# A three-layer block in split fp32r: sums over later keys as two fp32r passes, high passes first after a norm, another order of the feed-forward and of the first loads

## The reference

```python
z = einsum("bqhd,bkhd->bhqk", q, k) * scale
log_beta = log_sigmoid(z)
log_fail = where(s_idx < t_idx, log_beta - z, 0.0)          # = -softplus(z)
survive = cumsum(log_fail, axis=3, reverse=True) - log_fail # sum over later keys
a = where(s_idx < t_idx, exp(log_beta + survive), 0.0)
o = einsum("bhqk,bkhd->bqhd", a, v)
```

```python
u, g = split(rms_norm(h) @ w_up_gate)
u = causal_dwconv(u, conv_w_ffn)          # three taps over tokens
ffn = (gelu(u) * g) @ w_down
```

## Time and profile before

| | us |
|---|---|
| median of 3 runs | 868.92 (868.86 to 870.4) |
| the profiled execution, its own time | 868.39 |
| its span, first to last instruction | 866.6 |
| PE busy | 841.5 |
| DVE busy | 613.7 |
| ACT busy | 490.8 |
| POOL busy | 145.1 |

### The profile page before, as it was taken

One profiled execution on the slowest core, in us unless ns is written; L12 is line 12 of the kernel. 1 busy time (PEld: TensorE's weight loads), 2 busy tenths in 40 slices (PEclk: granted clock), 3 DMA queues, 4 the chain that ended last, 5 costly groups with the idle time before them and its releaser, 6 DMA issues.

```text
span 866.6 us, 16776 instructions
## 1 busy us (share of the span) xinstructions
PE 841.5 (97%) x6768; PEld 803.8 (93%) x6768; DVE 613.7 (71%) x1004; ACT 490.8 (57%) x814; POOL 145.1 (17%) x151
## 2 busy tenths in 40 slices
PE   7999999999999999999999999789999999999996
PEld 6999999999999989999999999789999999888886
DVE  6647787886666686767764478797887697568754
ACT  6345556445444565555564458558777555346654
POOL 0000000000000333333341121335434011000002
PEclk9999999999999999999999999899999999999998
DMA  9654424436666524665566624435544376654431
GB/s 338 210 153 128 158 98 158 135 112 180 192 178 190 175 87 155 194 187 181 174 193 215 191 82 155 163 124 176 183 147 154 115 217 184 186 171 143 123 98 49
DMA packets 39853, 139.81 MB, mean 161 GB/s; under 512 B 4432, under 2 KB 5600, under 8 KB 39648
## 3 DMA queue, kind: packets, MB, share of 16 engines
q1 hardware_dynamic: 37728, 135.71, 49.8%
q10 hardware_dynamic: 2048, 3.02, 1.0%
HBM read 137.65 MB, written 1.06 MB: 160 GB/s over the span
## 4 chain that ended last, share of the span: by engine, by line
PE 79%; DVE 12%; ACT 4%; POOL 3%; issue 1%; DMA 1%; DVEq 0%; SPq 0%; ACTq 0%; POOLq 0%
PE ps L1593 62%; PE ps L1596 5%; DVE weights_lo L984 4%; PE ps L1618 3%; PE ps L1690 1%; DVE arena L1204 1%; DVE arena L1176 1%; PE ps L1680 1%; POOL arena L441 1%; PE ps L1705 1%; PE ps L1960 1%; PE ps L1942 1%; DMA raw_weights<-weights_in 1%; DVE x_lo L1171 1%; POOL arena L462 1%
## 5 line engine op out<-in xcount | busy, mean ns | idle before, releaser
L1593 PE MATMUL ps<-x_hi,weights_hi 128*128 128x256 f32 (+3 forms) x1288 | 374.5, 291 | 6.3 <-DVE x_lo L999 2.8
L984 DVE TENSOR_TENSOR weights_lo<-raw_weights,weights_hi 128x1024 fp32r<-128x1024 f32 x252 | 311.7, 1241 | 92.9 <-ACT weights_hi L549 92.8
L1593 PE MATMUL ps<-x_lo,weights_hi 128*128 128x256 f32 (+3 forms) x1288 | 364.6, 283 | 0.0
L1593 PE MATMUL ps<-x_hi,weights_lo 128*128 128x256 f32 (+3 forms) x1288 | 364.1, 283 | 0.0
L549 ACT ACTIVATE weights_hi<-raw_weights 128x1024 fp32r<-128x1024 f32 x252 | 264.8, 1053 | 163.5 <-issue 71.0
L1593 PEld LDWEIGHTS ps<-x_hi,weights_hi 128*128 128x128 f32 x1288 | 244.1, 190 | 14.3 <-issue 7.0
L1593 PEld LDWEIGHTS ps<-x_lo,weights_hi 128*128 128x128 f32 x1288 | 244.3, 190 | 1.0 <-issue 0.7
L1593 PEld LDWEIGHTS ps<-x_hi,weights_lo 128*128 128x128 f32 x1288 | 244.4, 190 | 0.0
L1593 PE MATMUL ps<-y_hi,weights_hi 128*128 128x256 f32 (+1 forms) x488 | 137.8, 282 | 1.4 <-POOL y_lo L445 1.4
L1593 PE MATMUL ps<-y_lo,weights_hi 128*128 128x256 f32 (+1 forms) x488 | 137.4, 282 | 0.0
L1593 PE MATMUL ps<-y_hi,weights_lo 128*128 128x256 f32 (+1 forms) x488 | 137.1, 281 | 0.0
(11 more groups left out here) (230 smaller groups left out, 1075.0 us busy)
## 6 DMA issues: line engine op xcount, KB each, us to landing
raw_weights<-weights_in SPq DMA_DIRECT2D x252, 512.0 KB, 3.7
arena<-decay_rows ACTq DMA_DIRECT2D x8, 256.0 KB, 3.9
masks<-masks_in SPq DMA_DIRECT2D x1, 1379.0 KB, 11.0
hidden<-xT_in SPq DMA_DIRECT2D x2, 272.0 KB, 3.6
hidden<-xT_in SPq DMA_DIRECT2D x1, 544.0 KB, 6.2
raw_weights<-weights_in SPq DMA_DIRECT2D x2, 256.0 KB, 4.3
out<-arena SPq DMA_DIRECT2D x4, 128.0 KB, 2.2
out<-arena ACTq DMA_DIRECT2D x4, 128.0 KB, 2.1
```

The costliest lines, as they stand in the source:

```text
L984: d.sig(TT(wlo[:, s * CW:(s + 1) * CW], raw[:, (c % RAW) * CW:(c % RAW + 1) * CW], whi[:, s * CW:(s + 1) * CW].bitcast(F32), ALU.subtract) ...
L1593: ins = mm(bank(BANK_OF[no])[:, 0:b - a], wt, x_[:, kt, a:b], start=s0, stop=s1)
```

## The change

Six edits, in one kernel:

1. **Sums over later keys.** ACT casts softplus(z) to fp32r (`fail_high`), DVE subtracts (`fail_low`), and `survive` runs the three matmuls twice, over the high and the low parts, for both heads of a pair in one call. The two matrices of -1, also as fp32r, are cast once by ACT from the masks. The new buffers lie in a part of `y_hi` and `y_lo` that is used only later.
2. **Softplus ahead of the convolution.** In DVE's program `fail` moves to before tile h is taken out, `fail_low` stands after it, before the convolution. The causal mask is multiplied only into the 320 columns (two times 160) that can hold an edge.
3. **High passes first.** `project_together` waits for the high part of a k-tile, runs the two passes over it for its three tiles, then waits for the low part and runs the third pass for the three.
4. **Totals later.** `total(2, TA)` and `total(3, META)` move from k-tile 3 to k-tile 7.
5. **Feed-forward.** Tiles 0 and 1 go through each step together; from tile 2 on DVE takes u of tile i and adds its taps before it multiplies tile i-1, and ACT and POOL are ordered to match.
6. **Beginning.** x goes on ACT's queue, weights on SP's; chunks 1 to 3 are issued once the first half of chunk 0 has landed; chunk 1 too is split in halves; k-tiles 2 and 3 of x are split before the second half of chunk 0. Masks come in two loads, "identity", "ones" and two constants before chunk 4, the rest before chunk 8. PE warms up with six matmuls instead of three, on a buffer of 256 columns that POOL sets first.

```diff
         @block.sync
-            load_x(0)
             sp_.dma_start(raw[:, 0:half], weights[0, :, 0:half]).then_inc(S("load_half"), 16)
-            load_x(1)
             sp_.dma_start(raw[:, half:CW], weights[0, :, half:CW]).then_inc(S("raw0"), 16)
-            load_x(2)
+            sp_.wait_ge(S("load_half"), 16)
             for c in range(1, NCHUNKS):
                 if c == RAW:
-                    sp_.dma_start(msk[:], masks).then_inc(S("load_masks"), 16)
+                    sp_.dma_start(msk[:, 0:EARLY_MASKS], masks[:, 0:EARLY_MASKS]).then_inc(S("load_masks"), 16)
+                if c == 2 * RAW:
+                    sp_.dma_start(msk[:, EARLY_MASKS:MASK_COLS], masks[:, EARLY_MASKS:MASK_COLS]).then_inc(
+                        S("load_late_masks"), 16)
...
         @block.gpsimd
+            g.sig(nc.gpsimd.memset(aw[:, 0, 0:L], 1.0), "zeroed")
...
+            ffn_scale(0)
+            ffn_scale(1)
+            ffn_low(0)
+            ffn_low(1)
+            for i in range(2, FT):
+                ffn_scale(i)
+                if i > 2:
+                    ffn_low(i - 1)
+            ffn_low(FT - 1)
...
         @block.scalar
+            load_x(0)
+            act.dma_start(prm[:], params).then_inc(S("load_params"), 16)
+            load_x(1)
+            load_x(2)
             exp_and_ln()
-            act.dma_start(prm[:], params).then_inc(S("load_params"), 16)
...
+            def fail_high(p):
+                for e in range(2):
+                    act.wait_ge(S("f_ready"), 2 * p + e + 1)
+                    a.sig(A(f_hi[:, e, :], fz[:, e, :], ACT.Copy), "f_hi")
...
                 softplus_part(p)
                 feed(("h", p))
+                fail_high(p)
                 if p:
                     att_high(p - 1)
...
+            for i in range(2, FT):
+                ffn_tap(i)
+                feed(("fu", i))
+                ffn_gelu(i)
+                if i > 2:
+                    ffn_high(i - 1)
+                feed(("fg", i))
+            ffn_high(FT - 1)
...
         @block.vector
+                edge = two_edges(arena, fz_at + (h % 2) * ZC)
+                d.sig(TT(edge, edge, two_edges(msk, MASKS["stick"][0]), ALU.mult), "f_ready")
...
+            def fail_low(p):
+                for e in range(2):
+                    dve.wait_ge(S("f_hi"), 2 * p + e + 1)
+                    d.sig(TT(f_lo[:, e, :], fz[:, e, :], f_hi[:, e, :].bitcast(F32), ALU.subtract), "f_lo")
...
                 feed(("c", p))
+                fail(2 * p)
+                fail(2 * p + 1)
                 r = result(("h", p), 0, T - TC)
...
                 feed(("h", p))
-                fail(2 * p)
-                fail(2 * p + 1)
+                fail_low(p)
...
+            ffn_up(0)
+            ffn_up(1)
+            ffn_conv(0)
+            ffn_conv(1)
+            feed(("fu", 1))
+            ffn_out(0)
+            ffn_out(1)
+            feed(("fg", 1))
+            for i in range(2, FT):
+                ffn_up(i)
+                if i > 2:
+                    feed(("fg", i - 1))
+                ffn_conv(i)
+                if i > 2:
+                    ffn_out(i - 1)
+                feed(("fu", i))
+            ffn_out(FT - 1)
+            feed(("fg", FT - 1))
...
         @block.tensor
+                    ready_hi(kt)
+                    for passes in (((whi, hi), (wlo, hi)), ((whi, lo),)):
+                        if len(passes) == 1:
+                            ready_lo(kt)
+                        for tile, (a, b) in zip(tiles, spans):
...
-            pe.wait_ge(S("zeroed"), 2)
-            for _ in range(3):
-                mm(bank(6)[:, 0:L], vals[:, 2, 0:P], vals[:, 2, 0:L], start=True, stop=True)
+            pe.wait_ge(S("zeroed"), 1)
+            for _ in range(6):
+                mm(bank(6)[:, 0:L], aw[:, 0, 0:P], aw[:, 0, 0:L], start=True, stop=True)
...
+                for n, part in enumerate((f_hi, f_lo)):
+                    for e in range(2):
+                        pe.wait_ge(S("f_lo" if n else "f_hi"), 2 * p + e + 1)
+                        zb, f_ = bank(4 + e), part[:, e, :]
...
+                        mm(zb[:, 0:ZC], at_or_later, f_, start=False, stop=False, skip_group_check=True)
+                        mm(zb[:, 128 - TA:NA], later, f_[:, c1:c2], start=False, stop=False, skip_group_check=True)
+                        ins = mm(both, later, f_[:, c2:ZC].unsqueeze(1).to_broadcast([P, 2, ZC - c2]), start=False,
+                                 stop=n == 1, skip_group_check=True)
...
-            project(("fg", 1), xhi, xlo, META, T, lambda kt: total(2, TA) if kt == 3 else None)
+            project(("fg", 1), xhi, xlo, META, T, lambda kt: total(2, TA) if kt == KT - 1 else None)
...
-            project(("ex", 0), xhi, xlo, META, T, lambda kt: total(3, META) if kt == 3 else None)
+            project(("ex", 0), xhi, xlo, META, T, lambda kt: total(3, META) if kt == KT - 1 else None)
```

More of the change, by code:

```diff
@@ L201, in build @@
         CONV, ATT, MERGED = 0, 1, 2
+        spare = MERGED * KT * NA
+        f_hi, f_lo = v3(yhi_t[:, spare:spare + 2 * ZC], 2), v3(ylo_t[:, spare:spare + 2 * ZC], 2)
+        later = yhi_t[:, spare + 2 * ZC:spare + 2 * ZC + P]
+        at_or_later = yhi_t[:, spare + 2 * ZC + P:spare + 2 * ZC + 2 * P]
         def mask(name):
@@ L436, in _, with ffn_scale @@
             add_normed(0, TA)
-            for i in range(FT):
+            def ffn_scale(i):
                 pool.wait_ge(S("gelu_ready"), i + 1)
@@ L583, in _ @@
             a.sig(A(whi[:, 0:half], raw[:, 0:half], ACT.Copy), "hi_half")
-            first_high(0)
-            first_high(1)
+            for kt in range(4):
+                first_high(kt)
             act.wait_ge(S("raw0"), 16)
             a.sig(A(whi[:, half:CW], raw[:, half:CW], ACT.Copy), "hi_ready")
-            nxt[0] = 1
-            for kt in range(2, KT):
+            for kt in range(4, KT):
                 first_high(kt)
-            for _ in range(RING - 1):
+            act.wait_ge(S("raw1"), 16)
+            a.sig(A(whi[:, CW:CW + half], raw[:, CW:CW + half], ACT.Copy), "hi_half")
+            a.sig(A(whi[:, CW + half:2 * CW], raw[:, CW + half:2 * CW], ACT.Copy), "hi_ready")
+            nxt[0] = 2
+            for _ in range(RING - 2):
                 split_hi()
@@ L612, in _ @@
                     take_values_of(i - 1)
+            act.wait_ge(S("load_late_masks"), 16)
+            a.sig(A(later, mask("neg_ones"), ACT.Copy), "neg_masks")
+            a.sig(A(at_or_later, mask("neg_tri"), ACT.Copy), "neg_masks")
+            def fail_high(p):
+                for e in range(2):
+                    act.wait_ge(S("f_ready"), 2 * p + e + 1)
+                    a.sig(A(f_hi[:, e, :], fz[:, e, :], ACT.Copy), "f_hi")
             def softplus_part(p):
@@ L692, in _, with ffn_tap, ffn_gelu @@
             nc.scalar.preload_act_table_set("gelu_apprx_tanh_and_others")
-            for i in range(FT):
-                if i > 1:
-                    feed(("fu", i))
+            def ffn_tap(i):
                 act.wait_ge(S("u_ready"), i + 1)
                 a.sig(A(fcv[:, i % 2, :], fu[:, i % 2, 0:L], ACT.Copy, scale=pcol("conv_ffn", i)), "tap_ready")
-                if i == 0:
-                    feed(("fu", 1))
-                elif i > 1:
-                    feed(("fg", i))
+            def ffn_gelu(i):
                 act.wait_ge(S("u_conv"), i + 1)
@@ L1192, in _, with ffn_up @@
             dve.wait_ge(S("rms_ready"), 3)
-            for i in range(FT):
-                u, c_ = fu[:, i % 2, :], fcv[:, i % 2, :]
+            def ffn_up(i):
                 r = result(("fu", i), 0, NA)
@@ L1601, in project, with project_together @@
                         ins.then_inc(S("chunk_read"), 1)
-            def project_together(tiles, hi, lo, spans, ready, after=None):
+            def project_together(tiles, hi, lo, spans, ready_hi, ready_lo, after=None):
                 for tile in tiles:
@@ L1992 @@
 MASK_COLS = 0
-for _name, _n in (("identity", P), ("ones", L), ("neg_ones", P), ("neg_tri", P), ("stick", ZC), ("stick_neg", ZC),
-                  ("causal", CC), ("causal_neg", CC), ("restart", L), ("chunk", L), ("eps", 1), ("one", 1)):
+for _name, _n in (("identity", P), ("ones", L), ("eps", 1), ("one", 1), ("neg_ones", P), ("neg_tri", P), ("stick", ZC),
+                  ("stick_neg", ZC), ("causal", CC), ("causal_neg", CC), ("restart", L), ("chunk", L)):
     MASKS[_name] = (MASK_COLS, _n)
     MASK_COLS += _n
+EARLY_MASKS = MASKS["neg_ones"][0]
 ARENA = 17600
```

129 lines of the change are left out of this document (70 added, 59 removed).

## The result

| | before | after |
|---|---|---|
| median of the runs, us | 869.29 (868.86 to 870.4, 4 runs) | 858.11 (856.69 to 858.4, 4 runs) |
| ratio, 95% interval | | 0.9866 (0.9849 to 0.9883) |
| profiled execution, span | 868.39, 866.6 | 856.69, 854.9 |
| mean granted clock in it | 0.992 | 0.996 |

Faster by 11.2 us, where 11.75 was forecast (857.1, in the range 852.5 to 863.5). Executions of the changed kernel end near 856.7 or, more often, near 858.0, by whether PE's clock falls behind one wait or not (experiment 10); the profiled one is of the first kind, so 11.7 us are to be found between the two traces, and 11.2 between the medians.

The account below looks back on a forecast made before the run. PE was taken as the bound, busy 841.5 us, 97% of the span. Gains of 5.2 + 2.0 + 4.55 + 0 = 11.75 from 868.39 gave 856.6, or 857.1 by the median; range 852.5 to 863.5.

Parts of the forecast that it names:

- Part 1: Mixer's sums over later keys: twelve fp32r matmuls replace six fp32, 2.35 to 1.70 us a pair, 5.2 in eight.
- Part 2: Beginning: x and weights on separate queues, k0 ends near 9.8, full clock kept; 2.0 us, bounds 0.6 and 2.6.
- Part 3, passes: First three tiles together after the first norm: only three matmuls stand behind the last low part, gain 0.9 us.
- Part 3, first total's wait: First norm: the total moved from k-tile 3 to 7 drops its wait, 0.55 us.
- Part 3, order of the tiles less the new wait: Feed-forward: the new order removes three waits, 0.9 + 1.0 + 1.6, less 0.4 for fu3's weights' remainder; 3.1 us.
- second norm: Same edits would give 0.7 + 0.6 there, counted 0: the inverse norm comes when it did, PE waits longer.
- the floor (b): Sums over later keys: every matmul's weight load sets a floor, 0.19, 0.117 and 0.117, a pair 1.70 us.
- Rivals A and B: Narrow fp32r no faster than fp32, 861.1, chance 0.20 (A); at column rate, weight load hidden, 852.9, chance 0.13 (B).
- The cover of 1.5 us: Mixer lap: the pair's weights are ready at +13.9, needed by the next scores at 15.4; 1.5 us are over.
- rival C: Mixer: DVE and ACT set the lap, which grows by 1.0 + 1.1; slower, 879, chance 0.05.
- My bound, in which a half-clock stretch costs 1.4: Beginning, lower bound 0.6 us: the half-clock stretch stays, 12 x (0.24 - 0.125) = 1.4 lost.
- my sign, waits grown by 1.3 behind 546: Layer 3, around 546 to 549: PE's waits should have grown by about 1.3 us.

Follow-up runs that it names:

- experiment 10: Changed kernel plus four matmuls of ones, result unread, in PE's wait ahead of layer 3's second gate projection: 856.86 us, ratio 0.9858.
- experiment 2: Changed kernel with the sums over later keys back as six fp32 matmuls, no casts or remainders, DVE's new order kept: 862.49 us.
- experiment 12: Changed kernel with the old order of the beginning and four matmuls of ones in PE's wait at 532: 858.6 us.
- experiment 9: Changed kernel with the old order of passes in the three projections that run together: 857.91 us.
- experiment 7: Changed kernel with both totals back at k-tile 3: 858.33 us.
- experiment 6: Changed kernel with the feed-forward in the old order of tiles on DVE, ACT and POOL: 861.36 us.
- experiment 11: Kernel before the change with only total(3) moved from the fourth k-tile to the last: 868.16 us against 869.26, ratio 0.9991.
- experiment 4: Changed kernel with one more unread 64-column fp32r matmul per pass and head, 32 in all: 860.95 us.
- experiment 3: Changed kernel with DVE's softplus sums back behind tile h, the two fp32r passes kept: 860.48 us.
- experiment 8: Changed kernel with the parameters' transfer issued ahead of x's first part on ACT's queue: 857.96 us.

## Why the prediction was right

| term | forecast | measured | by |
|---|---|---|---|
| Part 1, sums over later keys | 5.2 | 5.5 | ledger, experiment 2 |
| Part 2, beginning | 2.0 | 1.2 (1.7 in experiment 12) | ledger |
| Part 3, passes | 0.9 | 0.4 | experiment 9 |
| Part 3, first total's wait | 0.55 | 0 | experiment 7 |
| Part 3, order of the tiles less the new wait | 3.1 | 3.8 (4.5 when undone alone) | ledger, experiment 6 |
| second norm | 0 | 0.8 | experiments 7, 11 |
| sum | 11.75 | 11.7 between traces, 11.2 between medians | |

The main part and its mechanism came true. That the sum agrees to 0.05 is luck: the beginning, the passes and the first total's wait were 1.85 too high together, and the mixer, the order of tiles and the second norm 1.8 too low. (The range given for the forecast, 855 to 861, does not quite follow either: parts 2 and 3 by their own bounds give 856.1 to 860.6.)

**Part 1** went as forecast, by the reason given. The choice among three bounds decided it, and the floor (b), found at transposes and at a 32-column load in another precision, held: 0.17 to 0.20, 0.11 and 0.11 against 0.19, 0.117 and 0.117. What I had not seen is the re-entry of 0.09, which I counted in the old pair and not in the new; it was offset by the twelve matmuls, 1.57 instead of 1.70. Rivals A and B fall with the pair's 1.66 and with experiment 4. The gap formula of the Trainium skill (TensorE: Matmul & The Clock Gate, Back-to-back issue gap) is not followed by these narrow fp32r matmuls: 0.11 for 64 columns, where it would give 0.03. That section calls it the gap of an isolated matmul and says that it under-counts narrow matmuls in a stream with weight loads; the traces agree. The cover of 1.5 us that I named against rival C was real: the pair's weights are done 1.55 us before the scores start (94.15 against 95.70), and experiment 3, where the scores wait for them, shows that the order makes it.

**Part 2** was too high. I had ACT casting the first half chunk by 5.0; it began at 5.5, held by the parameters, whose transfer I had counted as an issue and not as a landing. But experiment 8 shows that this was not the step that failed: with the parameters early the first total is no earlier. What failed is the landing of x. I had the first half of k0's x cast by 6.7 and the rest by 9.0; with the parameters out of the way ACT still waits for x at 5.38 and 6.65, and in the changed kernel and in experiment 8 its last cast of x ends near 9.95. PE took up k0's second half at 9.78, where I had k0's end, and began k1 at 11.53 instead of 10.2: 1.4 earlier than before (12.90), not 2.6.

What carried this 1.4 is the weights' remainder of chunk 1, of which DVE has a first half at about 11.4 in the changed kernel and which it has whole only at about 12.7 in the kernel before (the first of the three merged here):

```profile
11.49 3.50 DVE L984 TENSOR_TENSOR weights_lo<-raw_weights,weights_hi 128x1024 fp32r<-128x1024 f32 x3 [0.25 <-ACT weights_hi L549]
```

```profile
10.78 1.29 DVE L1062 TENSOR_TENSOR weights_lo<-raw_weights,weights_hi 128x512 fp32r<-128x512 f32 x2
```

So with the old order full clock alone would have let k1 begin 0.2 us sooner at most, an estimate from these rows (no run has the halved chunk alone); in the trace of experiment 11, which has the same beginning as the kernel before, PE waits 0.33 for that remainder and begins k1 at 13.15. My bound, in which a half-clock stretch costs 1.4, was therefore wrong on both sides: it cost about 0.2 in the kernel before, and 0.4 in the new one (experiment 3, where the next wait took it up).

Full clock was kept, but my reason for it was wrong and it held by luck. I had idle times under 1.2; the wait ahead of k0 was 1.75 in the profiled execution and 0.87 to 1.87 in the ten traces with the new beginning. The clock fell in one of them, behind the 1.87, while the old order shows half-rate matmuls (0.226 us apart) in all its four traces, behind waits of 1.40 to 1.71 (in that of experiment 11 the granted clock reads 1.00 all the same).

**Part 3** had the right sum for the feed-forward from wrong shares. *Passes*: I had the end three matmuls behind the last low part, DVE giving one each 1.28 us. In the trace the last low part comes only 1.65 us after the one two k-tiles earlier (309.6), not 2.56, so behind that one PE has 21 matmuls to do and sets the end itself: 309.63 to 312.24 without a wait. *Total*: its wait went, and PE met the weights of tile fu 3, 0.56 late; I had counted that wait once, at 0.4, against all terms together, and it is what the total's 0.55 turned into. *Order of tiles*: the three waits are all gone; I summed them as they stood, but PE that arrives 1.2 us earlier at them would have waited longer, so undoing the order costs 4.5.

POOL's scaling is slower in the new order. The groups of its instructions in the feed-forward, before and after (count, busy, mean ns, idle before):

```profile
L441 POOL TENSOR_TENSOR arena<-arena,rinv 128x256 f32<-128x256 f32 x20 | 15.3, 763 | 60.9 <-ACT arena L704 60.9
```

```profile
L443 POOL TENSOR_TENSOR arena<-arena,rinv 128x256 f32<-128x256 f32 x21 | 31.9, 1518 | 60.0 <-ACT arena L736 59.8
```

The same scaling takes 1.52 instead of 0.76 us, while POOL's low part became faster, 0.88 instead of 1.20 on the mean. The order is the cause: experiment 6, the changed kernel with the old order, has 0.76 and 1.20 again. The timelines show what runs beside: in the new order the scaling falls together with DVE's remainder of a weight chunk and the low part comes when DVE waits; in the old one it is the other way round.

```profile
346.17 1.53 POOL L443 TENSOR_TENSOR arena<-arena,rinv 128x256 f32<-128x256 f32 x1 [3.00 <-ACT arena L736]
347.84 0.73 POOL L449 TENSOR_TENSOR y_lo<-arena,y_hi 128x256 fp32r<-128x256 f32 x1
```

DVE's remainder stands there at 345.89 to 347.1, and DVE then waits until 348.67. The Trainium skill (GPSIMD Engine Reference, Specifications) says that GpSimd shares its SBUF interface with VectorE and contends with its instructions of two SBUF inputs; the traces agree, as the remainder is such an instruction. The slower scaling costs nothing here, since no wait of the feed-forward ends on POOL any more.

**Second norm**: here a step of mine was wrong. I reasoned that the inverse norm comes when it did, so that PE's lead must turn into a longer wait. But the total's matmuls in the old place held PE until the squares were there, and DVE's and ACT's chain of layer 3 passes through PE's own work, the extra block, the low ranks and the transposes; with PE earlier the chain is earlier. The chain of waits of the changed kernel shows it (start, us, what), tile ex 1 of the extra block and then the low ranks:

```profile
511.18 3.08 PE ps L1680 x24
514.26 1.74 PE ps L1874 x8
```

The wait of 3.0 us has the same length in both traces, and my sign, waits grown by 1.3 behind 546, did not come. The high passes gave nothing at this norm (experiment 9), so the 0.8 is the total's place alone, which I had at 0.6.

## What to carry to other kernels

Price a narrow split matmul by the weight load beside it, not by its columns, and read its price over a whole group, since printed starts bunch up. Two edits can be worth 5.5 together and 0 and 1.9 apart: shorten what bounds a lap and see at once which engine's order bounds it next. A wait that goes is worth its length only if the next feeder is as early, so sum waits with PE's new arrival times; and before a lead is written off at a long wait, follow the chain that ends it back to see whether it passes through the engine itself.

## What was not expected of the hardware

PE's clock fell to half after single waits of 1.4 to 1.9 us, in some executions of a kernel and not in others with nearly the same waits: behind the wait up to 9.23 in the earlier trace rows, behind the 1.87 us ahead of k0 in experiment 3, behind the 1.81 at 534, and not behind the 1.75 and 1.78 us of the profiled execution of the changed kernel. At the wait of 3.0 us in layer 3 it fell in all fourteen traces, also in that of the kernel before, where only the stretch near the beginning was named:

```profile
558.00:565.50 7.50, 6.33 (x30) 6.15 (x32) 7.15 (x10) 5.31 (x12) 5.75 (x6) 0.54 0.50 175
```

A fall lasted 3.4 us, and some 7 in this trace and in that of experiment 3. What it costs hangs on what follows: nothing where the wait for POOL takes it up, 0.4 in experiment 3, and 1.5 us behind the wait at 534. This last one makes the two kinds of execution of the changed kernel, and four idle matmuls in that wait took the slower kind away: 858.0 to 856.9. The scatter of the kernel before, 867.7 to 870.5, is not explained by it: its executions with the higher mean clock are not the shorter ones.
